# Long convolution: the forward transform and half the spectrum one pass earlier, filter sizes summed at another place, the last inverse in two rounds

## The reference

```python
def hyena_filters(L, w1, b1, w2, b2, w3, b3, freq):
    ...
    h = (hid @ _f32(w3) + _f32(b3)).reshape(L, HY_ORDER, 2, HY_WIDTH)
    ...
    h = h * jnp.exp(-t * jnp.abs(deltas))[:, None, None, :]
    fwd, bwd = h[:, :, 0], h[:, :, 1]
    kern = jnp.concatenate([fwd, jnp.zeros((1, HY_ORDER, HY_WIDTH), jnp.float32), bwd[:0:-1]], axis=0)
    kern = kern / jnp.sum(jnp.abs(kern), axis=0, keepdims=True)
    return jnp.fft.rfft(kern, axis=0)

def long_conv(u, k_f, skip):
    L = u.shape[1]
    uf = _f32(u)
    y = jnp.fft.irfft(jnp.fft.rfft(uf, n=2 * L, axis=1) * k_f, n=2 * L, axis=1)[:, :L]
    return (y + uf * _f32(skip)).astype(u.dtype)

def hyena_mixer(...):
    ...
    z = parts[0]
    for o in range(HY_ORDER):
        z = parts[o + 1] * long_conv(z, k_f[:, o], skip[o])
    return (z * jax.nn.silu(gate)) @ w_out
```

## Time and profile before

| what | value |
|---|---|
| median of 3 runs (lowest, highest) | 4877.11 us (4876.91, 4878.86) |
| the profiled execution, its span | 4874.79 us, 4873.0 us |
| busy over the span: TensorE, VectorE, ScalarE, GpSimd | 4188.9, 1900.1, 1097.4, 258.3 us |
| mean granted clock of TensorE over the span | 0.928 |
| the long convolution's stage in the span | 1834 to 2421 us |

### The profile page before, as it was taken

The page is one execution under the profiler, slowest core; times in us unless marked ns, Lnnn a source line. Parts: engine busy times, 40 slices in busy tenths (PEclk is TensorE's granted clock), DMA queues, the critical chain, the costliest instruction groups (busy, mean ns, idle before and its releaser), DMA issues. The chain is left out here.

```text
span 4873.0 us, 59321 instructions
## 1 busy us (share of the span) xinstructions
PE 4188.9 (86%) x20951; PEld 2145.5 (44%) x20951; DVE 1900.1 (39%) x2969; ACT 1097.4 (23%) x1816; POOL 258.3 (5%) x368
## 2 busy tenths in 40 slices
PE   5899799998999998999589988877999599949995
PEld 1454455554444445777444435532333244413331
DVE  1233344443312205898635927441111333321112
ACT  0122355442111112222011236310000235100000
POOL 0100000000000000111000000000000200000001
PEclk7899899999999998999799989988999799969998
DMA  8122221113454511111150112226864511366666
GB/s 322 42 68 59 54 51 38 37 44 123 141 195 181 211 59 48 54 54 53 66 185 13 52 67 82 70 90 261 341 254 182 187 29 49 104 264 239 248 236 259
DMA packets 255619, 622.86 MB, mean 128 GB/s; under 512 B 70915, under 2 KB 149333, under 8 KB 235649
## 3 DMA queue, kind: packets, MB, share of 16 engines
q1 hardware_dynamic: 219786, 504.86, 29.3%
q0 software_dynamic: 19424, 94.01, 5.1%
q10 hardware_dynamic: 16280, 22.27, 1.3%
HBM read 1293.97 MB, written 113.53 MB: 289 GB/s over the span
## 5 line engine op out<-in xcount | busy, mean ns | idle before, releaser
L1720 PE MATMUL hyp_acc<-hy_hT,hyp_early_weights 128*128 128x512 f32 x768 | 334.9, 594 | 0.0
L3498 PE MATMUL blocks_h<-moe_w,blocks_xT 128*32 128x512 f32 x2560 | 292.7, 610 | 42.1 <-issue 42.1
L3498 PE MATMUL blocks_h<-od_hT,blocks_xT 128*32 128x512 f32 x1280 | 291.0, 608 | 26.1 <-DMA moe_w1b<-in_ex_w 21.0
L3519 PE MATMUL blocks_acc<-moe_w,blocks_hidT 128*32 128x512 f32 x2560 | 284.8, 597 | 11.5 <-DMA moe_w<-in_ex_w 10.2
L3498 PE MATMUL blocks_h<-moe_w1b,blocks_xT 128*32 128x512 f32 x1280 | 291.0, 608 | 0.0
L1045 PE MATMUL att_scores<-att_kT,att_qT 64*128 64x512 f32 (+3 forms) x768 | 252.0, 548 | 21.3 <-DMA att_v<-scratch_V 21.3
L2284 PE MATMUL evp_acc<-ev_hT,evp_early_weights 128*128 128x512 f32 x512 | 224.7, 600 | 7.6 <-DVE evp_qkT L2425 5.6
L981 DVE TENSOR_REDUCE att_nmax<-att_scores 128x1 f32<-128x1280 f32 x128 | 190.2, 1486 | 102.0 <-PE att_scores L1045 102.0
L1069 PE MATMUL att_turn<-ident,att_probs 128*128 128x128 f32 x1280 | 193.0, 281 | 41.5 <-DVE att_o L1011 22.5
L1720 PEld LDWEIGHTS hyp_acc<-hy_hT,hyp_early_weights 128*128 128x128 f32 x768 | 144.7, 191 | 173.6 <-issue 173.5
L949 ACT ACTIVATE att_probs<-att_scores,att_nmax 128x1280 f32<-128x1280 f32 x128 | 169.9, 1327 | 173.9 <-DVE att_nmax L981 171.9
(11 more groups left out here) (533 smaller groups left out, 6198.1 us busy)
## 6 DMA issues: line engine op xcount, KB each, us to landing
moe_w<-in_ex_w SPq DMA_DIRECT2D x320, 2048.0 KB
od_hT<-in_ex_w SPq DMA_DIRECT2D x80, 2048.0 KB
moe_w1b<-in_ex_w SPq DMA_DIRECT2D x80, 2048.0 KB
hyp_m_weights<-in_mod_w POOLq DMA_DIRECT2D x6, 8192.0 KB, 24.2
mod_weights<-in_ada_w SPq DMA_DIRECT2D x12, 2048.0 KB, 20.7
scratch_y_rows<-blocks_x ACTq DMA_DIRECT2D x40, 512.0 KB, 8.7
hyp_early_weights<-in_hy_w_in SPq DMA_DIRECT2D x8, 2048.0 KB
scratch_parts<-hyp_uT SPq DMA_DIRECT2D x24, 512.0 KB, 3.7
```

The source lines that it names most:

```text
L1720: mm = nc.tensor.matmul(acc[:, m % 2, half * NC:(half + 1) * NC], weights[:, ws, kt, c:c + P], hT[:, kt, half * NC:(half + 1) * NC], start ...
L3498: mm = nc.tensor.matmul(out[mine, :], xT[:, kt, mine], w[l][:, kt, :], start=(kt == 0), stop=(kt == KT - 1))
L3519: mm = nc.tensor.matmul(acc[mine, c, :], hidT[:, kt, mine], w2[l][:, kt, c * NC:(c + 1) * NC], start=(kt == 0), stop=(kt == FT - 1))
```

## The change

- TensorE, pass i: K(i+1), four tiles of filter i+2, a wait until VectorE has emptied them (`tiles_gone`), U(i+1) (before: U(i), first), the other four tiles, then r=0 to 3 with `norm(i+2)` ahead of r=3. U(0) is made in the prologue.
- The spectrum is cut into five parts (`spectra`: enter, multiply, combine, spread, leave) that write into a tile `work` instead of `xu`. For ft=0 of pass i+1 the first four are made in pass i: two ahead of the scalings, one each ahead of r=1 and r=2.
- Totals: two right behind the last filter tiles, two ahead of scaling r=1. Butterflies, reciprocal and size copy come between the two groups of filter tiles; the reciprocal is taken in the pass that uses it.
- Pass 7: the inverse runs in two rounds, over ft=0 for all r, then ft=1, in four banks (two of them `x_bank`); the product goes into `filt`. Part of its spectrum is made in pass 6.
- The skip weights are loaded 256 at a time (`load_skip`), the small tile `ktmp` is now part of `tmp`.

```diff
-        skip, skip_in = sb("skip", [1, PASSES * CCH]), sem("skip_in")
+        skip = sb("skip", [1, CCH])
...
-        tmp, ktmp = sb("tmp", [P, PH, 2, CCH]), sb("ktmp", [P, 2, 2, CCH])
+        tmp, work = sb("tmp", [P, PH, 2, CCH]), sb("work", [P, PH, 2, CCH])
+        ktmp = tmp[:, 0:2, :, :]
...
+        z_last = filt[:, :, :, :].rearrange("p (m r) v c -> p m r v c", r=PH)
...
+        def product_of(i):
...
+            return z_last if isinstance(i, int) and i == PASSES - 1 else z
...
+        def y_place(i, r):
...
+            return x_bank[r] if r >= 2 and isinstance(i, int) and i == PASSES - 1 else y_bank[r % 2]
...
+                def load_skip(j):
+                    sp.wait_ge(tapped, signals(j))
+                    sp.dma_start(skip[:, :], skips[:, bass.ds(j * CCH, CCH)]).then_inc(skip_in, 16)
+
+                load_skip(0)
...
                 sp.dma_start(inv[:, :, :, :, :], d["k_inv"]).then_inc(mats_in, 16)
+                load_skip(1)
...
                         load_u(i + 1)
+                    if ahead:
+                        load_skip(i + 2)
...
                 def filters(j, tiles):
                     for t in tiles:
                         b = t % PH
-                        if t < PH:
-                            if not isinstance(j, int) or j:
-                                pe.wait_ge(x_copied[b], signals(j * COPIES - MT))
-                        else:
+                        if not isinstance(j, int) or j:
+                            pe.wait_ge(x_copied[b], signals(j * COPIES - (MT if t < PH else 0)))
+                        if t >= PH:
                             pe.wait_ge(filt_ready, signals(j * NF + (t - PH + 1)))
                         nc.tensor.matmul(x_bank[b][:, :, :].rearrange("p v c -> p (v c)"), hid[:, t, :],
...
+                def u_transform(j):
+                    pe.wait_ge(u_in, signals(j * 16 + 16))
+                    transform(u_parts, lambda ft: u_copied(j, ft) - 1, u_made)
+
+                def tiles_gone(j):
+                    for b in range(PH):
+                        pe.wait_ge(filt_ready, signals(j * NF + (b + 1)))
...
                     k_transform(0)
-                    filters(1, range(NF))
+                    filters(1, range(PH))
+                    tiles_gone(1)
+                    u_transform(0)
+                    filters(1, range(PH, NF))
                     norm(1)
...
+                def last_inverse(i):
...
+                    for ft in range(MT):
+                        pe.wait_ge(z_made, signals(i * MT + (ft + 1)))
+                        for r in range(PH):
+                            if ft == 0:
+                                if r < 2:
+                                    pe.wait_ge(y_scaled[r], signals(i * (PH // 2)))
+                                else:
+                                    pe.wait_ge(x_copied[r], signals(i * COPIES + COPIES))
+                            for t in range(MT):
+                                for cs in range(2):
+                                    mm = nc.tensor.matmul(y_place(i, r)[:, t, :], inv[:, ft, r, cs, t * P:(t + 1) * P],
+                                                          product_of(i)[:, ft, r, cs, :],
+                                                          start=(ft == 0 and t == 0 and cs == 0),
+                                                          stop=(ft == MT - 1 and t == MT - 1 and cs == 1))
+                            if ft == MT - 1:
+                                mm.then_inc(y_made, 1)
...
                 def body(i, more, ahead):
+                    if not more:
+                        return last_inverse(i)
                     if more:
                         pe.wait_ge(filt_ready, signals(i * NF + 2 * NF))
-                    pe.wait_ge(u_in, signals(i * 16 + 16))
-                    transform(u_parts, lambda ft: u_copied(i, ft) - 1, u_made)
-                    if more:
                         k_transform(i + 1)
                     if ahead:
                         filters(i + 2, range(PH))
+                        tiles_gone(i + 2)
+                    if more:
+                        u_transform(i + 1)
+                    if ahead:
+                        filters(i + 2, range(PH, NF))
                     pe.wait_ge(z_made, signals(i * MT + MT))
                     for r in range(PH):
-                        if ahead and r == 1:
-                            filters(i + 2, range(PH, NF))
                         if ahead and r == PH - 1:
                             norm(i + 2)
                         pe.wait_ge(y_scaled[r % 2], signals(i * (PH // 2) + r // 2))
                         for t in range(MT):
                             last = gather(y_bank[r % 2][:, t, :], [
-                                (inv[:, ft, r, cs, t * P:(t + 1) * P], z[:, ft, r, cs, :])
+                                (inv[:, ft, r, cs, t * P:(t + 1) * P], product_of(i)[:, ft, r, cs, :])
                                 for ft in range(MT) for cs in range(2)])
                         last.then_inc(y_made, 1)
...
                 def copies(n, made, dst):
                     for ft in range(MT):
+                        if made is u_made and not (isinstance(n, int) and n == 0):
+                            act.wait_ge(xu_read, signals(n * MT + (ft + 1 - MT)))
                         for b in range(PH):
                             act.wait_ge(made, signals(n * NX + (ft * PH + b + 1)))
                             nc.scalar.activation(dst[:, ft, b, :, :], x_bank[b][:, :, :], ACT.Copy).then_inc(x_copied[b], 1)
...
                     k_copies(0)
                     decays(1)
+                    copies(0, u_made, xu)
                     sizes(1)
...
-                    act.wait_ge(z_made, signals(i * MT))
-                    copies(i, u_made, xu)
                     if more:
                         k_copies(i + 1)
                     if ahead:
                         decays(i + 2)
+                    if more:
+                        copies(i + 1, u_made, xu)
+                    if ahead:
                         sizes(i + 2)
...
                 def k_butterfly(j, ft):
                     x = xk[:, ft, :, :, :]
                     dve.wait_ge(x_copied[PH - 1], signals(k_copied(j, ft)))
-                    dve.wait_ge(z_made, signals(j * MT))
+                    if not (isinstance(j, int) and j == 0):
+                        dve.wait_ge(z_made, signals((j - 1) * MT + (ft + 1)))
...
+                def spectra(i, ft, parts):
...
+                    links = Chain(dve, u_steps, i * (MT * U_STEPS) + ft * U_STEPS)
+                    x, k, w = xu[:, ft, :, :, :], vk[:, ft, :, :, :], work[:, :, :, :]
+
+                    def enter():
+                        dve.wait_ge(x_copied[PH - 1], signals(u_copied(i, ft)))
+                        dve.wait_ge(vk_ready, signals(i * MT + MT))
+                        dve.wait_ge(z_made, signals(i * MT + ft))
+                        tt(tmp[:, 0:2, :, :], x[:, 0:2, :, :], x[:, 2:4, :, :], ALU.add)
+                        tt(tmp[:, 2:4, :, :], x[:, 0:2, :, :], x[:, 2:4, :, :], ALU.subtract).then_inc(xu_read, 1)
+                        dve.wait_ge(xu_read, signals(i * MT + (ft + 1)))
+                        links.link(turn(nc.vector, tmp[:, 0, :, :], tmp[:, 1, :, :], tmp[:, 2, :, :], tmp[:, 3, :, :], w, 1))
+
+                    def multiply():
+                        links.n = 1
+                        links.link(tt(tmp[:, :, :, :], w, k, ALU.mult))
+                        tt(w[:, :, 0, :], w[:, :, 0, :], k[:, :, 1, :], ALU.mult)
+                        links.link(tt(w[:, :, 1, :], w[:, :, 1, :], k[:, :, 0, :], ALU.mult))
+
+                    def combine():
+                        links.n = 3
+                        links.link(tt(tmp[:, :, 0, :], tmp[:, :, 0, :], tmp[:, :, 1, :], ALU.subtract))
+                        links.link(tt(tmp[:, :, 1, :], w[:, :, 0, :], w[:, :, 1, :], ALU.add))
+
+                    def spread():
+                        links.n = 5
+                        tt(w[:, 0:2, :, :], tmp[:, 0:2, :, :], tmp[:, 2:4, :, :], ALU.add)
+                        links.link(tt(w[:, 2:4, :, :], tmp[:, 0:2, :, :], tmp[:, 2:4, :, :], ALU.subtract))
+
+                    def leave():
+                        if product_of(i) is z:
+                            dve.wait_ge(y_made, signals(i * PH))
+                        turn(nc.vector, w[:, 0, :, :], w[:, 1, :, :], w[:, 2, :, :], w[:, 3, :, :],
+                             product_of(i)[:, ft, :, :, :], 3).then_inc(z_made, 1)
+
+                    for part in parts:
+                        (enter, multiply, combine, spread, leave)[part]()
...
-                    for ft in range(MT):
-                        k_butterfly(0, ft)
-                    filters(1, range(NF))
+                    k_butterfly(0, 0)
+                    filters(1, range(PH))
+                    k_butterfly(0, 1)
```

(79 more changed lines are left out.)

## The result

The changed kernel takes 4847.14 us (median of 4 runs, 4842.56 to 4852.2) against 4877.98 (4 runs, 4876.91 to 4879.31): ratio 0.9939, interval 0.9928 to 0.9951, so 30.8 us or 0.6% less. Run a second time with the experiments it took 4844.23 against 4874.9, 30.7 less (0.9929, 0.9916 to 0.9943).

What follows compares the result with a forecast made beforehand. TensorE was taken as the bound, with VectorE nearly as full, so reordering could win at most 6.8 us a pass. Loop 20.1, fill -5.3 and last passes 20.4 sum to 35.2 us saved: 4842 us, range 4832 to 4858.

Steps and rivals of the forecast that it cites:

- The loop: Five passes K(2) to K(7): period 61.4 us against 65.43, 4.0 won a pass, 20.1 us in all.
- Wait one: TensorE stands in `tiles_gone` after its four filter tiles, before U(i+1), until VectorE has emptied them: 1.33 us a pass.
- Wait two: TensorE's size sum, after r=2 of the inverse, waits for VectorE's last totals: 1.4 us a pass.
- three signs of being wrong: Granted clock below 1.00 in the loop, GpSimd collisions above 1.1 us, or ScalarE's decays released later than 21.9 us.
- Collisions at 1.1: VectorE instructions beside GpSimd's product: each collision costs 1.1 us, within bounds of 0 and 2.25.
- rival 1: VectorE's chain longer than counted, collisions at 2.25 us: period 63.6, 11 us less won, 4853 us; chance 0.12.
- The fill: Prologue from K(0) to K(2): K(2) at 1988.5 us instead of 1983.16, 5.3 us lost.
- The last two passes: From K(7) to the last scaling: 82.3 us instead of 102.74, 20.4 us won.
- The saving goes through whole: Behind the edited stage: last plane's store and next stage follow as before, so all 35.2 us reach the total.
- 2 (short pauses lower the clock): Rival: TensorE's two short waits each cost 1.9 us once; period 63.9, 4859 us; chance 0.05.
- 3: Rival: wait in `tiles_gone` holds TensorE at the lower clock through U and second tiles; period 77.2, 4921 us; chance 0.04.
- 4: Rival: loop gains nothing, a VectorE wait leaves about 65.4 us a pass, only fill and tail remain; 4862 us; chance 0.07.

Runs made afterwards that it cites:

- e4: Changed kernel with GpSimd's product of y and the next part cut to 4 of 256 columns: 4843.41 us, ratio 0.9932.
- e5: Changed kernel, prologue reordered: enter and multiply ahead of filter tiles 4 to 7, combine and spread behind the totals: 4835.49 us, ratio 0.992.
- e1: Changed kernel with the last inverse back in one round, r by r after both halves of the spectrum: 4851.67 us, ratio 0.9953.
- e3: Changed kernel with reciprocal and size copy back at the end of the pass before: 4856.2 us, ratio 0.9962.
- e2: Changed kernel with the totals back one r later each, ahead of scaling r=1 and r=2: 4884.22 us, ratio 1.0014.
- e6: e5 with, in the loop, the last two totals ahead of combine, combine one round later, spread behind tap: 4833.59 us, ratio 0.9908.
- e7: e6 with the inverse's r=0 made between the four filter tiles and U, and scaled ahead of enter: 4838.07 us, ratio 0.9919.

## Why the prediction came out as it did

The forecast was 4842 us (4832 to 4858), measured were 4847.14 and 4844.23. The mechanism held in its three parts; the sizes came out so:

- **The loop** (61.4 a pass): right to 0.16, step by step. The filter tiles, the release of the size sum (54.51 after K, foreseen 54.49) and the period are where the walk put them. Wait one measured 1.38 (foreseen 1.33). Wait two measured 0.94 (foreseen 1.4): TensorE came to it 0.47 later, by 0.22 at U's start (half of it the release, 0.23 instead of the assumed 0.12) and by joints behind it; VectorE came when foreseen. Two of the three signs of being wrong came, both small: the loop's granted clock was 0.99, as one U started at 0.50, and the filter tiles ran 0.09 later than ScalarE's decays were to release them.
- **Collisions at 1.1:** 1.07 at leave and spread, 0.95 at combine. e4 shows that the product causes them. It is not a constant, though: a VectorE instruction with both inputs in SBUF that starts inside the product loses what is left of the product, less 0.14 (the last scalings, with one input in PSUM, take 0.69 inside it as elsewhere). The Trainium skill, "SBUF — State Buffer", section "Who interferes with whom", says so: whichever of the two issues first has the shared ports for its whole instruction, and the other is blocked until then. The trace agrees, in both directions: the product alone takes 1.26, and 2.18 where a VectorE instruction had started 0.16 before it. So the 2.25 that rival 1 took as a bound was GpSimd's own time in such a wait, and 1.1 fitted because the new order's VectorE instructions follow one another as closely as those of its row.
- **The fill** (5.3 lost) was mis-sized: 6.6. Two terms: U(0) started 0.44 later after K(0) than counted, and the size sum behind its 4.20 wait took 6.12 to tap instead of the 5.63 taken from the earlier trace rows; that is 0.93 of the 1.3, the rest lies in joints. The mechanism is what e5 removed. The prediction's "nothing over it" is too strong: K(1) and four tiles run meanwhile, and what counts is that VectorE's chain outlasts them, and TensorE waits 13.83 us for it.
- **The last two passes** (20.4 won): 21.2. The old 28.39 wait became one of 4.84. The spectrum ended 0.35 sooner, as its four collisions cost 3.9 instead of 4.4, and the round with its last scaling was 0.4 shorter. e1 gives the two rounds 6.95 of it.
- **"The saving goes through whole":** in the profiles 33.95 of stage, in the medians 30.8 and 30.7. The difference of 3 is inside the scatter of the rest, 9.7 us over the profiles, but no run shows that it is only that.
- **The rivals.** 1 (longer chain) did not come. 2 (short pauses lower the clock) came in one pass of five and cost 0.23 there, as its price for a U that hides in wait two (0.6) allows. But the experiments show how near it was: e3 paid 1.5 a pass for it, e2 1.7 at the size sum alone, and e4 and e6 lost to it most of what they won in the loop. The forecast's case held because wait one met a clock that mostly stayed, and nothing in the profile of before could tell that; the one row with 1.26 us was thin evidence. That part was luck. 3 did not come: after a slow start the clock rose within each U. 4 is e2's outcome, and worse: with the totals late the loop's whole gain is gone. No run undoes U's new place or the early half of the spectrum alone, so how the gain divides among them is not shown.

Open is what decides whether U keeps the clock. Its wait alone does not: after 1.38 us it stayed at the full level in all six waits of e5, in four of the changed kernel's five and in none of e2's five. In the fill, behind one and the same wait of 1.54 and the same work ahead, U(0) took 14.05 us in the changed kernel (both profiles), e4 and e7, and 17.05 to 17.07 in e1, e2, e3 and e6. The chip alone does not decide it, since e6 and e7 ran on one chip with one prologue. One thing orders the nine profiles, e5 among the slow: the size sum ahead of K(0), which starts at the lower level (granted clock 0.50 over its first 2 us) behind a wait of 4.20. It took 5.17 to 6.44 us in the four fast ones and 6.48 to 6.73 in the five slow. That is an order seen afterwards, with 0.04 us between the groups; no run tests it. The changed kernel, then e1:

```profile
1853.20 6.44 PE L1959 MATMUL lc_n_bank<-lc_total,lc_early_ones 128*128 128x256 f32 x16 [4.20 <-DVE lc_total L2142]
...
1850.13 6.49 PE L1959 MATMUL lc_n_bank<-lc_total,lc_early_ones 128*128 128x256 f32 x16 [4.20 <-DVE lc_total L2140]
...
1883.82 17.06 PE L1959 MATMUL lc_x_bank<-lc_u,lc_early_fwd 128*128 128x256 f32 x64 [1.54 <-DVE lc_filt L2124]
```

The Trainium skill, "TensorE: Matmul & The Clock Gate", section "A second HAM failure mode: psum-queue depth-cycling", has the clock swing where TensorE idles briefly and often between groups of products; that fits e4, e6 and e7, where it swings between passes; it does not say which pass is hit, and no run here does.

## What to carry to other kernels

Walk one pass of the new order engine by engine, with durations from rows that have the same neighbours; that gave both waits of the loop to within half a us. Price a meeting of VectorE and GpSimd by what is left of the instruction that came first, not by a flat figure. When two engines are both at 97%, removing one's small wait mostly moves it, and on TensorE a wait of 1.4 to 2.6 us can also cost 1.5 to 3 us of slow restart, so count restarts beside waits. Ask of each prologue whether it has the same order as the loop: the cheapest 8 us here lay in half a spectrum that could run in time when VectorE stood idle.

## What the runs showed that was not expected

- The same kernel's stages behind the edit differ by 6.3 us between two profiles (2459.99 and 2466.34), with steps of about 3 us at different stages. A single pair of profiles can't place a loss of that size.
- Two lengths of one transform, 14.05 and 17.05 us, behind the same instructions and the same wait of 1.54 us.
- Leaving out nearly all of GpSimd's product (36 us of busy time in the loop) left the loop 0.2 us a pass shorter.
